# Expert biases: from a product on TensorE to a broadcast on GpSimd and an addition on VectorE

## What is computed

```python
def expert_block(args):
    xb, e = args
    gu = xb @ w_gate_up[e] + b_gate_up[e]
    gate = jnp.minimum(gu[:, 0::2], SWIGLU_LIMIT)
    up = jnp.clip(gu[:, 1::2], -SWIGLU_LIMIT, SWIGLU_LIMIT)
    act = (up + 1.0) * gate * jax.nn.sigmoid(SWIGLU_ALPHA * gate)
    return act @ w_down[e] + b_down[e]
```

## Time and profile before

| | us |
|---|---|
| median of three runs | 1783.71 |
| lowest, highest | 1783.46, 1787.79 |
| the profiled execution | 1785.83 |
| its span in the trace | 1784.1 |
| TensorE busy | 1684.0 |
| DVE busy | 561.4 |
| ACT busy | 312.6 |
| POOL busy | 174.2 |

### The profile page before, as it was taken

One profiled execution on the slowest core, in us unless ns is written; L12 is line 12 of the kernel. 1 busy time (PEld: TensorE's weight loads), 2 busy tenths in 40 slices (PEclk: granted clock), 3 DMA queues, 4 the chain that ended last, 5 costly groups with the idle time before them and its releaser, 6 DMA issues.

```text
span 1784.1 us, 42867 instructions
## 1 busy us (share of the span) xinstructions
PE 1684.0 (94%) x18523; PEld 876.8 (49%) x18523; DVE 561.4 (31%) x1266; ACT 312.6 (18%) x677; POOL 174.2 (10%) x250
## 2 busy tenths in 40 slices
PE   5999897689999968999999999999999999999997
PEld 2444796366478854434434434434434434434433
DVE  3679444664134465212112112111111111211211
ACT  3142322455222220100100100100100100100100
POOL 4000520101000030000100100100100000000000
PEclk9999999899999987999999999999999999999999
DMA  9950000401141267999999999999999999999992
GB/s 332 340 209 1 3 4 4 171 1 49 47 141 48 96 245 268 361 393 395 378 394 401 388 388 394 384 392 394 387 391 393 384 392 397 386 391 397 388 388 62
DMA packets 98343, 489.58 MB, mean 274 GB/s; under 512 B 15131, under 2 KB 17240, under 8 KB 48997
## 3 DMA queue, kind: packets, MB, share of 16 engines
q1 hardware_dynamic: 88326, 471.06, 67.6%
q0 software_dynamic: 7504, 16.80, 4.1%
q10 hardware_dynamic: 2448, 0.78, 0.2%
HBM read 478.87 MB, written 19.28 MB: 279 GB/s over the span
## 4 chain that ended last, share of the span: by engine, by line
PE 61%; DVE 0%; issue 0%; POOLq 0%; ACT 0%; DVEq 0%
PE bank L2061 37%; PE bank L2072 18%; PE bank L2046 1%; PE bank L2085 1%; PE bank L2052 1%; PE bank L2073 1%; PE bank L2062 1%; PE bank L2095 0%; DVE sb_y L2245 0%; POOLq L1953 0%; DVE sb_mod L2236 0%; DVE sb_mod L2230 0%; DVE sb_xT L2220 0%; ACT sb_mod L2155 0%; DVE sb_aT L2225 0%
## 5 line engine op out<-in xcount | busy, mean ns | idle before, releaser
L2061 PE MATMUL bank<-sb_w_raw,sb_xT 128*32 128x512 f32 x4608 | 666.4, 593 | 0.0
L2062 PE MATMUL bank<-sb_w_raw,sb_xT 128*32 128x512 f32 x1536 | 666.0, 593 | 0.0
L2061 PEld LDWEIGHTS bank<-sb_w_raw,sb_xT 128*32 128x32 f32 x4608 | 186.1, 110 | 453.3 <-issue 453.3
L2072 PE MATMUL bank<-sb_w_raw,sb_aT 128*32 128x256 f32 x4608 | 337.9, 379 | 2.0 <-DVE sb_aT L2226 2.0
L2073 PE MATMUL bank<-sb_w_raw,sb_aT 128*32 128x256 f32 x1536 | 337.5, 380 | 0.0
L2072 PEld LDWEIGHTS bank<-sb_w_raw,sb_aT 128*32 128x32 f32 x4608 | 187.7, 110 | 130.8 <-DVE sb_y L2245 2.3
L2230 DVE TENSOR_SCALAR sb_mod<-bank 128x256 f32<-128x256 f32 x96 | 40.2, 418 | 626.9 <-ACT sb_mod L2155 626.9
L2073 PEld LDWEIGHTS bank<-sb_w_raw,sb_aT 128*32 128x32 f32 x1536 | 166.3, 110 | 0.0
L2062 PEld LDWEIGHTS bank<-sb_w_raw,sb_xT 128*32 128x32 f32 x1536 | 166.1, 110 | 0.0
L2155 ACT ACTIVATE sb_mod<-bank 128x256 f32<-128x256 f32 x96 | 29.9, 384 | 660.8 <-PE bank L2062 660.8
L2245 DVE SCALAR_TENSOR_TENSOR sb_y<-bank,sb_prob_now,sb_mod 96x256 f32<-96x256 f32 x96 | 40.4, 474 | 234.5 <-PE bank L2073 234.5
(11 more groups left out here) (441 smaller groups left out, 1956.3 us busy)
## 6 DMA issues: line engine op xcount, KB each, us to landing
sb_w_raw<-in_w_gate_up_dram SPq DMA_DIRECT2D x256, 1024.0 KB, 11.1
sb_w_raw<-in_w_down_dram SPq DMA_DIRECT2D x128, 1024.0 KB, 12.9
sb_ring<-in_w_in_dram SPq DMA_DIRECT2D x7, 2048.0 KB, 10.6
sb_x<-in_ada_w_dram SPq DMA_DIRECT2D x8, 1024.0 KB, 9.2
sb_mod<-in_ada_w_dram SPq DMA_DIRECT2D x8, 1024.0 KB, 9.6
sb_ring<-in_ada_w_dram SPq DMA_DIRECT2D x3, 2048.0 KB, 14.7
sb_x<-in_x_dram SPq DMA_DIRECT2D x2, 2048.0 KB, 13.9
sb_ring<-in_w_out_dram SPq DMA_DIRECT2D x2, 2048.0 KB, 7.9
```

Source lines behind the costliest of these rows:

```text
L2061: te.matmul(up_bank[r][at, :], g.xT[:, k, at], g.w_raw[:, s, 512 * r:512 * r + 512], start=False, stop=last)
L2062: mm = te.matmul(up_bank[r][CAP:P, :], g.xT[:, k, STRIP * r:STRIP * r + STRIP], g.w_raw[:, s, 512 * G:2048], start=False, stop=last)
L2072: te.matmul(down_bank[j][at, 0:256], g.aT[:, k, at], g.w_raw[:, s, 1024 * r + 256 * j:1024 * r + 256 * j + 256], start=first, stop=last)
```

## The change

The bias becomes a row in SBUF that is spread over the partitions. `phase_route` loads the biases once (32 partitions), adds 1 to the up ones, and writes them to a table in DRAM, `bias_rows`; the split into two parts, its ACT copy, its DVE subtraction and POOL's pattern go. In the loop SP loads one row of 8 KB into `bias_row` ahead of a turn's weights, and waits for POOL's last `spread` first. POOL's `spread` consists of two partition broadcasts (1536 and 512 numbers to 128 partitions). ACT's `quarter` copies the last quarter into partitions 96 to 127. DVE's `added` adds three times 128 x 512 from PSUM and `g.bias` into the new tile `biased`, from which `gated` and `clipped` now read. TensorE's `bias_rows` goes; the first `up` opens the accumulation. The core of the diff:

```diff
+def load_bias(g, sp, e):
+    sp.dma_start(g.bias_row[0:1, :], g.bias_rows[e, :]).then_inc(g.row_in, 16)
...
-            for i in range(2):
-                sp.dma_start(g.bias_raw[N_EXP * i:N_EXP * i + N_EXP, :, :], g.a["b_gate_up"][0][:, 0:512 * G].rearrange("e (s n) -> e s n", s=G)).then_inc(bias_in, 16)
-                at = slice(64 + N_EXP * i, 64 + N_EXP * i + N_EXP)
-                for j in range(G):
-                    sp.dma_start(g.bias_raw[at, j, :], g.a["b_gate_up"][0][:, 512 * G:]).then_inc(bias_in, 16)
+            sp.dma_start(g.bias_raw[:, :], g.a["b_gate_up"][0]).then_inc(bias_in, 16)
             for t in ts:
...
+            sp.wait_ge(*vec.at("bias_up"))
+            sp.dma_start(g.bias_rows[:, :], g.bias_raw[:, :]).then_inc(g.bias_out, 16)
             sp.wait_ge(*vec.at("tab"))
             sp.wait_ge(*pe.at("lgT"))
             sp.wait_ge(g.h2_out, 16 * NT)
+            sp.wait_ge(g.bias_out, 16)
+            load_bias(g, sp, slice(0, 1))
             second = sp.value_load(g.table[0:1, 2:3], min_val=0, max_val=N_EXP - 1)
...
-            po.memset(g.pick[:, :], 0.0).then_inc(*pool("pick0"))
-            po.wait_ge(*pool.at("pick0"))
-            po.memset(g.pick[0:64, 0:CAP], 1.0).then_inc(*pool("pick1"))
-            po.wait_ge(*pool.at("pick1"))
-            po.memset(g.pick[64:P, CAP:P], 1.0).then_inc(*pool("pick2"))
-            po.wait_ge(*pool.at("pick2"))
             po.memset(g.x_slot[:, :], 0.0).then_inc(*pool("x_slot"))
...
-            sc.wait_ge(*vec.at("bias_up"))
-            sc.copy(g.bias[:, :, :], g.bias_raw[:, :, :]).then_inc(*act("bias_hi"))
...
-            ve.wait_ge(bias_in, 16 * (2 + 2 * G + NT))
-            up = g.bias_raw[:, :, :].rearrange("p s (n a) -> p (s n) a", a=2)[:, :, 1]
+            ve.wait_ge(bias_in, 16 * (1 + NT))
+            up = g.bias_raw[:, :].rearrange("p (n a) -> p n a", a=2)[:, :, 1]
             ve.tensor_scalar(up, up, 1.0, None, ALU.add).then_inc(*vec("bias_up"))
...
-            ve.wait_ge(*act.at("bias_hi"))
-            for i in range(2):
-                at = slice(64 * i + N_EXP, 64 * i + 2 * N_EXP)
-                ve.tensor_tensor(g.bias[at, :, :], g.bias_raw[at, :, :], g.bias[at, :, :].bitcast(F32), ALU.subtract).then_inc(*vec(f"bias_lo{i}"))
...
+            second = sp.value_load(g.table[0:1, 2:3], min_val=0, max_val=N_EXP - 1)
+            sp.wait_ge(*pool.credit())
+            load_bias(g, sp, bass.ds(second, 1))
+            rest_of_turn(0, sp.value_load(g.table[0:1, 1:2], min_val=0, max_val=N_EXP - 1), second)
...
             with sp.Fori(1, last) as turn:
                 e, after = expert(turn), expert(turn + 1)
+                sp.wait_ge(*pool.before("spread", turn))
+                load_bias(g, sp, bass.ds(after, 1))
                 for k in range(SPARE):
...
-            def bias_rows():
-                for b in range(G):
-                    mm = te.matmul(up_bank[b][:, :], g.bias_pick[:, :], g.bias[:, b, :], start=True, stop=False)
-                return mm
             def up(s, k):
-                last = k == UP - 1
+                first, last = k == 0, k == UP - 1
                 for r in range(G):
                     for c in range(G):
                         at = slice(STRIP * c, STRIP * c + STRIP)
-                        te.matmul(up_bank[r][at, :], g.xT[:, k, at], g.w_raw[:, s, 512 * r:512 * r + 512], start=False, stop=last)
-                    mm = te.matmul(up_bank[r][CAP:P, :], g.xT[:, k, STRIP * r:STRIP * r + STRIP], g.w_raw[:, s, 512 * G:2048], start=False, stop=last)
+                        te.matmul(up_bank[r][at, :], g.xT[:, k, at], g.w_raw[:, s, 512 * r:512 * r + 512], start=first, stop=last)
+                    mm = te.matmul(up_bank[r][CAP:P, :], g.xT[:, k, STRIP * r:STRIP * r + STRIP], g.w_raw[:, s, 512 * G:2048], start=first, stop=last)
...
-            te.wait_ge(*first_vec.at("bp0"))
-            bias_rows().then_inc(*first_pe("bias"))
...
-                te.wait_ge(*vec.before("bp", turn))
-                bias_rows().then_inc(*pe("bias"))
...
+            def quarter():
+                return sc.copy(g.bias[CAP:P, :, :], g.last_quarter[CAP:P, :].unsqueeze(1).broadcast_to([STRIP, G, 512]))
             def gated(b):
-                gate = up_bank[b][:, :].rearrange("p (n a) -> p n a", a=2)[:, :, 0]
+                gate = g.biased[:, b, :].rearrange("p (n a) -> p n a", a=2)[:, :, 0]
...
+            sc.wait_ge(*pool.credit())
+            quarter().then_inc(*first_act("quarter"))
             for b in range(G):
+                sc.wait_ge(*first_vec.at(f"ad{b}"))
                 gated(b).then_inc(*first_act(f"gc{b}"))
...
-                sc.wait_ge(*done(UP_DONE, turn))
+                sc.wait_ge(*pool.at("spread", turn))
+                sc.wait_ge(*vec.before("ad2", turn))
+                quarter().then_inc(*act("quarter"))
                 sc.wait_ge(*vec.before("ac2", turn))
                 for b in range(G):
+                    sc.wait_ge(*vec.at(f"ad{b}", turn))
                     gated(b).then_inc(*act(f"gc{b}"))
...
+            def spread():
+                po.partition_broadcast(g.bias[:, :, :].rearrange("p b n -> p (b n)"), g.bias_row[0:1, 0:512 * G])
+                return po.partition_broadcast(g.last_quarter[:, :], g.bias_row[0:1, 512 * G:])
             last = last_job(po)
+            po.wait_ge(g.row_in, 16)
+            spread().then_inc(*pool.credit())
...
+                po.wait_ge(g.row_in, 16 * turn + 32)
+                po.wait_ge(*vec.before("ad2", turn))
+                po.wait_ge(*act.before("quarter", turn))
+                po.wait_ge(ticked, 3 * turn + 1)
+                tick(2)
+                spread().then_inc(*pool("spread"))
                 po.wait_ge(*vec.at("row", turn))
-                po.wait_ge(ticked, 2 * turn + 1)
+                po.wait_ge(ticked, 3 * turn + 2)
                 tick(0)
                 gather_rows(g, po, g.row[0:CAP, 0:1])
...
-            def bias_pick(job):
-                return ve.tensor_scalar(g.bias_pick[:, :], g.pick[:, :], g.job_of[:, job], None, ALU.mult)
...
+            def added(b):
+                return ve.tensor_tensor(g.biased[:, b, :], up_bank[b][:, :], g.bias[:, b, :], ALU.add)
             def clipped(b):
-                ups = up_bank[b][:, :].rearrange("p (n a) -> p n a", a=2)[:, :, 1]
+                ups = g.biased[:, b, :].rearrange("p (n a) -> p n a", a=2)[:, :, 1]
...
+            ve.wait_ge(*first_act.at("quarter"))
+            ve.wait_ge(used[UP - 1], 1)
+            for b in range(G):
+                added(b).then_inc(*first_vec(f"ad{b}"))
...
-                ve.wait_ge(*pe.at("bias", turn))
-                bias_pick(bass.ds(turn + 2, 1)).then_inc(*vec("bp"))
+                ve.wait_ge(*act.at("quarter", turn))
+                ve.wait_ge(*done(UP_DONE, turn))
+                for b in range(G):
+                    added(b).then_inc(*vec(f"ad{b}"))
```

39 lines of the change are left out of this document (18 added, 21 removed).

## The result

The changed kernel takes **1799.72 us** (median of 4 runs, 1797.91 to 1800.40); the kernel before, on the same chip, 1783.72 us (4 runs, 1783.46 to 1787.79). The ratio is 1.0078, with a 95% interval from 1.0064 to 1.0092: slower by 16 us, 1.7 us beyond the forecast of 1798. The profiled run has a span of 1798.2 us; that of before has 1784.1.

What follows compares the result with a forecast made beforehand. TensorE bounds the turn by a hair beside full DMA engines; afterwards a 34.3 us ring would. From 1785.8: 3.1 and 2.6 saved, 20.2 added, 1800.3; less 2.1 against the median, 1798 us, range 1767 to 1885.

Steps and rivals of the forecast that it cites:

- The ring of one turn: Loop chain through POOL, ACT and DVE: 14.1 us plus two code switches, so no turn shorter than 34.3 us.
- TensorE bounds the turn by a hair, the DMA engines are full: Loop before: TensorE sets the 33.55 us turn; DMA share is 1.01, with no idle time to give.
- the lead: Loop's weight loads: they land at least 18 us before their slot is needed, which can be used up once.
- 0.87 us go from a turn, leaving 32.68: TensorE's turn head: removing the bias products takes 0.87 us from 33.55, leaving 32.68.
- 3.1 us at the start: First job and turn 0: removing the bias products saves 1.56 us in each, 3.1 together.
- The prices: New work per turn: ACT's `quarter` 1.48 us, DVE's three `added` 686 ns each, POOL's `spread` 2.5 us.
- A switch at R = 10.1, the third near nothing: POOL's code switches between tick and broadcast: 10.1 us each, twice a turn; the third, at the loop's head, 0.1 us.
- The rival built on it: POOL's switch takes about 6 us: ring 26.1 us, time 1774 us; chance 0.34 together with Rival 1.
- SP's weight loads are queued behind the wait for the broadcast: SP's queue: it waits for `spread` before a turn's bias row, with all twelve weight loads behind; no price in the forecast.
- Rival 1: Ring hidden, DMA engines bound the loop; 7 us of lead used, 1774 us (1766 to 1786); chance 0.34 with the 6 us switch.
- Signs: Changed profile: SP bursts every 34 to 35 us, 10 us POOL gaps twice a turn, `added` awaiting `quarter`, TensorE awaiting DVE.
- three turns at 32.68 and 27 at +0.75: Loop sum: three turns at 32.68 save 2.6 us, the other 27 cost 0.75 each, 20.2 us.

Runs made afterwards that it cites:

- run 4: The kernel before with the loop's bias products and row pick left out, nothing in their place: 1768.25 us, ratio 0.9886.
- run 9: The kernel before without the loop's bias products and row pick, SP held to the end of the seventh slot: 1777.14 us, ratio 0.9944.
- run 1: The changed kernel with POOL's three tiny products a turn (ticks) made fills, the wait carried by a semaphore instruction: 1779.36 us, ratio 0.9954.
- run 6: The changed kernel with one more tiny product on POOL between a turn's two broadcasts, so one more switch each way: 2225.41 us.
- run 10: The changed kernel with two more broadcasts ahead of the real one, into tiles that nobody reads: 1890.93 us.
- run 2: The changed kernel with SP's wait for the broadcast and the bias row's load moved behind the gate/up loads: 1786.11 us, ratio 0.9994.
- run 7: The changed kernel with only half the gate/up columns loaded in the loop, the others keeping old weights: 1763.84 us.
- run 8: The changed kernel with the bias row requested by ACT after its quarter copy, so SP never waits for POOL: 1777.03 us, ratio 0.9935.
- run 12: The changed kernel with fills for POOL's tiny products and the bias row requested by ACT: 1777.35 us, ratio 0.9943.
- run 3: The changed kernel with fills for POOL's tiny products and the bias row loaded after the gate/up loads: 1773.48 us, ratio 0.9922.
- run 5: The kernel before, with only SP held each turn to the seventh slot's end before its eight gate/up loads: 1787.61 us, ratio 0.9999.

## Why the prediction came out right, and where it did not

**The time was right, by luck; the account is half right.** The ring of one turn that gave the 34.3 us is not the one that sets the turn, and three errors cancel. By its own steps:

- *TensorE bounds the turn by a hair, the DMA engines are full*: right, and it is the main fact of this kernel. Runs 4 and 9 show the hair: without the bias products TensorE takes 32.85 us a turn until the lead is used up, the loads take 33.56 on the mean in run 9, and before takes 33.55.
- *0.87 us go from a turn, leaving 32.68*: the products go, but the turn is 32.85 in every run that isn't held up. The transposes stood 0.63 us ahead of the bias products, and now 0.81 ahead of the gate/up product (786.87 to 787.68). The term is 0.70.

```profile
786.87 0.87 PE L2078 MATMUL bank<-sb_ident,sb_mod 128*128 128x128 f32 x6
787.68 0.63 PE L2054 MATMUL bank<-sb_w_raw,sb_xT 128*32 128x512 f32 x3
```

- *3.1 us at the start*: wrong, turn 0 gave 0.25 and the part ahead of it took 1.0. The removed products had stood where TensorE runs at the lower of its two clocks (granted clock 0.50) after a wait, and now the gate/up product stands there. PE in the first job, after and before:

```profile
687.43 1.08 PE L2054 MATMUL bank<-sb_w_raw,sb_xT 128*32 128x512 f32 x3 [0.70 <-issue]
...
688.25 1.11 PE L2054 MATMUL bank<-sb_w_raw,sb_xT 128*32 128x512 f32 x3
```

```profile
689.99 0.84 PE L2061 MATMUL bank<-sb_w_raw,sb_xT 128*32 128x512 f32 x3
...
690.66 0.60 PE L2061 MATMUL bank<-sb_w_raw,sb_xT 128*32 128x512 f32 x3
```

  The gate/up product starts 2.56 us earlier (1.66 of it because the expert phase itself began earlier in this run), but six of its groups take 0.82 to 0.86 us instead of 0.43, and by the down bias products (692.71 against 692.91) 0.2 us are left. The granted clock over 688 to 693 us is 0.75 in before (first line) and 0.50 in the changed kernel:

```profile
688.00:693.00 5.00, 4.97 (x33) 1.69 (x31) 1.17 (x4) 1.54 (x2) 2.51 (x2) 0.75 0.11 15
688.00:693.00 5.00, 5.00 (x27) 1.21 (x22) 0.00 (x0) 0.00 (x0) 1.64 (x1) 0.50 0.02 7
```

  Then the three additions (1.89 us) lie on the path to the first turn's head, which waits 4.12 us for DVE instead of 3.04. I had priced these additions in the loop and forgotten them here.
- *The prices*: `quarter` 1.47 (said 1.48), `added` 0.685 each (0.686), the broadcasts 2.5 together (2.5). Right, and of no weight.
- *A switch at R = 10.1, the third near nothing*: right in the sum. 8.9 one way and 11.4 the other are 20.3 us; 2R was 20.2. The third can't be seen: the third tick takes 0.72 instead of 0.20 us, but so does the fill in its place in run 1 (0.61 instead of 0.10), which has no such instruction. The nearest rows were the right ones: a small transfer behind full queues and a table load. The Trainium skill (GPSIMD Engine Reference, Instruction dispatch) gives approximately 6 us for freshly loaded code; run 6 agrees with its 5.7 us at a DMA share of 0.00, not with its 7.9 us at 0.36, and the changed kernel's 8.9 and 11.4 us, where the DMA engines are full, don't agree. The rival built on it had the switch too short for that reason. How the traffic lengthens a switch is not shown: I had written that the code comes past the busy engines, but in run 6 a switch of 5.7 us passes with none of their packets recorded.
- *The ring of 14.1 + 2R = 34.3 us*: the ring exists (run 10, run 6), but its fixed part is 12.7. Adding to row number are 4.4 us where I had 5.0 (810.75 to 815.11), the three ticks with gather and add 4.1 where I had 4.7 (793.76 to 797.85), and the four semaphores seem to be hidden in the rest. So the ring was 33.0 us: 0.15 over the free turn of 32.85 and 0.5 under before's, not 0.75 over it. This is **the step that failed**: the ring did not bind by itself. Runs 2, 7 and 8 point to it, where turns of 32.85 went on with both switches, but the switches are shorter there (7.1 and 9.0 us in run 2), and so is the ring. The changed kernel's own trace shows it, since DVE's additions wait for the end of TensorE's product and not for the broadcast and `quarter` (us in total, times, longest):

```profile
DVE sb_biased L2237 <- PE bank L2055: 469.7, 23, 21.1
DVE sb_biased L2237 <- ACT sb_bias L2144: 105.6, 5, 21.9
```

- *SP's weight loads are queued behind the wait for the broadcast*: said in one sentence, and given no price in the forecast. It is what the time went to. The hold throws away the lead (first slot: 5.3 us at turn 1, 2.3 at turn 5, 19 before), so only two turns ran at 32.85 instead of twenty or more. After that a turn takes 34.16 us, more than the loads' pace, because the wait closes a second ring, over two turns. It can be followed in the changed kernel's trace; these are means over turns 4 to 27, each step starting where the one above ends:

```
the seventh slot's product starts; the gate/up product ends            5.39 us
the first `added` starts                                               0.09
the row number is written                                              4.35
POOL's first tick starts (the switch back)                            11.47
gather, add, third tick, switch; the broadcast starts                 13.18
the second broadcast ends                                              2.48
SP issues the first gate/up load of a burst                            0.63
that burst's load for the seventh slot has landed                     30.52
its product starts, two turns later                                    0.04
sum                                                                   68.16
```

  Half of 68.16 is 34.08 us, the turn. In each of the 24 turns the product starts 0.04 us after the landing, and in 23 of them `added` starts within 0.1 us of the product's end, so there is no slack on this path. It needs all three parts: SP's wait for the broadcast, the two switches, and the 30.5 us that a load needs behind a full queue. Rival 1 had the use of the lead and the burning of the queue, but took it for a single loss; it comes back in every turn.
- *Signs*: SP's bursts every 34 us and the gaps twice a turn came as written. TensorE waits at the seventh slot for weights, not at the transposes, and `added` waits for TensorE in 23 cases and for `quarter` in 8, not the other way round. By its own test these two signs spoke for rival 1, with a gap that spoke against it. I had not thought of a case with long switches *and* a slack ring.

**Why the sum fitted**: three turns at 32.68 and 27 at +0.75 gave +17.6; measured are +11.6 over thirty turns. The start was to give 3.1 and took 0.75, and the end took 1.7, at the lower granted clock. The errors, -6.0, +3.9 and +1.7, cancel. That is luck, and so is it that the ring of one turn came out at 34.3 us where another one makes 34.1 us.

**The gain that is missing**, in turns of the traces: 30 turns at 0.70 are 21 us; run 4 has 19.0 of them (32.913 on the mean of turns 1 to 30, against 33.547), the lead paying. The changed kernel has -11.6. The 30.6 us between them go to the lead that is never there (run 9 against run 4: 33.315 against 32.913, 12 us) and to what the hold and the switches do together (33.934 against 33.315, 18.6 us). The first part is shown by run 9. Of the second, some 6 us come with what else the change brings (33.128 in run 12 against 32.913 in run 4): the row's own load, the broadcasts, the copy and the additions, which no run takes apart. The rest needs the hold and the switches together (without the switches 33.213, without the hold 33.197) and full DMA engines (run 7: 32.85), which are the three parts of the ring over two turns. Two things stay open: that the burst lengthens the switches is argued from the gaps of 8.9 and 11.4 us against 7.9 and 9.0 in run 8, and no run changed the burst alone; and no run stretched the ring over two turns without making that of one turn the longer.

The change in its best form (run 3) gains 0.8% (0.5 to 1.1); as written it loses 0.8.

## What to carry to other kernels

Where two engines are full, find out how far ahead the loads are, and what the change does to that lead: an engine that gets faster lives on it and then stops at the loads' pace, and a queue that is made to wait loses it at once. A wait for another engine's result ahead of the weight loads, in the queue that issues them, costs nothing as long as that lead isn't needed (run 5), and much once it closes a ring through the loads; put the small dependent load on an engine that knows anyway that the data is due (run 8). Look for rings that close over two turns too, and compare each with the free turn. On GpSimd keep operations between which it need not switch together in a loop, or replace the small ones by a kind that runs beside both, as the fill did in run 1.

## What the hardware showed that I had not expected

- A switch of GpSimd's code has no fixed price. To the broadcast it was 5.7 us at a DMA share of 0.00, and back 7.9 us at 0.36 (run 6). There and back it was 7.1 and 9.9 us at a share of 0.73 (run 7), 7.9 and 9.0 at full engines with loads issued one by one (run 8), and 8.9 and 11.4 with loads issued in bursts of twelve. From product to broadcast it was shorter than back in each run with two switches a turn.
- A fill on GpSimd needs no switch next to either kind, and an indirect DMA doesn't either (run 1: the fill and the broadcast start 0.07 us apart).
- Once the lead is gone, turns take 33.87, 33.72 and 33.83 us in runs 1, 3 and 12, where no code is loaded, against 33.56 in run 9. These three have the bias row's load in the loop, 8 KB of 13 MB onto one partition, but also the broadcasts, the copy and the additions. That it is the row is a guess; no run took it away alone.
- A hold of 20 us a turn on the queue of all weight loads was free, to within 0.1%, in a kernel whose DMA engines are full: their share was 0.99 to 1.00 with the hold and 1.01 without (run 5).
